# Gate/up pairs 1 to 8 with four seven-product steps, two of their four weight sums on GpSimd, and the last convolution transposes moved inside a step

## The reference

```python
h = rmsnorm(x, norm_mix)
q, k, v, o, i, f, cb, cc, cx, ga, gb = split(h @ w_in)
hm = sigmoid(o) * headnorm(mlstm_chunkwise(q, k, v, i, f)) * mh_norm   # 8 heads, chunks of 128
u = causal_depthwise_conv(cc * cx, conv_w)                             # 3 taps
merged = sigmoid(ga) * (hm @ w_branch_a) + sigmoid(gb) * ((cb * u) @ w_branch_b)
x = x + merged @ w_out
hf = rmsnorm(x, norm_ffn)
x = x + (silu(hf @ w_gate) * (hf @ w_up)) @ w_down                     # w_gate, w_up: 2048 x 5632
out = rmsnorm(x, norm_final)
```

## Time and profile before

| | |
|---|---|
| median of 3 runs | 1713.92 us |
| profiled execution, its own time | 1713.56 us |
| its span, first to last instruction | 1711.7 us |
| TensorE busy | 1698.0 us (99%), 7673 matmuls, granted clock 0.999 |
| VectorE, ScalarE, GpSimd busy | 1281.9, 888.0, 71.3 us |
| gate/up stage | from 1003.6 to about 1470 us of the span |
| DMA | 331.39 MB, mean 194 GB/s |

### The profile page before, as it was taken

The page is one execution under the profiler, slowest core; times in us unless marked ns, Lnnn a source line. Parts: engine busy times, 40 slices in busy tenths (PEclk is TensorE's granted clock), DMA queues, the critical chain, the costliest instruction groups (busy, mean ns, idle before and its releaser), DMA issues.

```text
span 1711.7 us, 20301 instructions
## 1 busy us (share of the span) xinstructions
PE 1698.0 (99%) x7673; PEld 1407.2 (82%) x7673; DVE 1281.9 (75%) x1108; ACT 888.0 (52%) x780; POOL 71.3 (4%) x65
## 2 busy tenths in 40 slices
PE   9999999999999999999999999999999999999998
PEld 7888888888878888888888888888888888888886
DVE  5888555566579998865554589888888888898987
ACT  6555544454455555553333465555555555665564
POOL 1000010101030000000000000000000000230000
PEclk9999999999999999999999999999999999999999
DMA  8555545554546555555556556665556655556653
GB/s 284 187 196 197 195 158 189 172 162 162 181 158 221 197 201 209 206 187 187 189 192 226 197 167 204 199 200 198 201 199 199 199 197 196 187 194 221 221 193 115
DMA packets 139185, 331.39 MB, mean 194 GB/s; under 512 B 8721, under 2 KB 8817, under 8 KB 138737
## 3 DMA queue, kind: packets, MB, share of 16 engines
q1 hardware_dynamic: 138976, 329.98, 57.2%
q10 hardware_dynamic: 144, 0.52, 0.1%
HBM read 328.38 MB, written 2.10 MB: 193 GB/s over the span
## 4 chain that ended last, share of the span: by engine, by line
PE 97%; DVE 1%; issue 1%; ACT 0%; DMA 0%; SPq 0%; POOLq 0%; DVEq 0%; POOL 0%; ACTq 0%
PE ps L1713 11%; PE ps L1714 11%; PE ps L1722 11%; PE ps L2032 9%; PE ps L2034 9%; PE ps L2038 9%; PE ps L1821 7%; PE ps L1814 7%; PE ps L1815 7%; PE ps L2113 4%; PE ps L2114 4%; PE ps L2118 4%; PE ps L1739 1%; PE ps L1988 1%; DVE w_lo L1064 0%
## 5 line engine op out<-in xcount | busy, mean ns | idle before, releaser
L1064 DVE TENSOR_TENSOR w_lo<-w_raw,w_hi 128x2048 fp32r<-128x2048 f32 x308 | 709.2, 2306 | 136.9 <-ACT w_hi L616 134.5
L616 ACT ACTIVATE w_hi<-w_raw 128x2048 fp32r<-128x2048 f32 (+1 forms) x309 | 588.8, 1909 | 291.2 <-PE ps L1714 102.8
L1713 PE MATMUL ps<-w_hi,xT_hi 128*128 128x512 f32 x448 | 179.6, 401 | 1.7 <-ACT w_hi L616 1.7
L1714 PE MATMUL ps<-w_hi,xT_lo 128*128 128x512 f32 x448 | 174.6, 390 | 0.0
L1814 PE MATMUL ps<-w_hi,xT_hi 128*128 128x512 f32 x426 | 165.9, 389 | 0.9 <-ACT w_hi L616 0.9
L1815 PE MATMUL ps<-w_hi,xT_lo 128*128 128x512 f32 x426 | 165.7, 389 | 0.0
L2032 PE MATMUL ps<-w_hi,fT_hi 128*128 128x512 f32 x396 | 156.2, 395 | 0.0
L2034 PE MATMUL ps<-w_hi,fT_lo 128*128 128x512 f32 x396 | 154.3, 390 | 0.0
L616 ACT ACTIVATE t_hi<-t_raw 128x1536 fp32r<-128x1536 f32 x45 | 66.9, 1486 | 110.3 <-PE ps L2038 87.8
L2038 PE MATMUL ps<-w_lo,fT_hi 128*128 128x512 f32 x396 | 120.1, 389 | 0.0
L1821 PE MATMUL ps<-w_lo,xT_hi 128*128 128x512 f32 x426 | 112.5, 390 | 0.4 <-DVE w_lo L1064 0.4
(11 more groups left out here) (344 smaller groups left out, 2801.9 us busy)
## 6 DMA issues: line engine op xcount, KB each, us to landing
w_raw<-in_w_in SPq DMA_DIRECT2D x127, 1024.0 KB, 5.0
w_raw<-in_w_gate SPq DMA_DIRECT2D x88, 512.0 KB, 3.8
w_raw<-in_w_up SPq DMA_DIRECT2D x88, 512.0 KB, 4.6
w_raw<-in_w_down SPq DMA_DIRECT2D x44, 1024.0 KB, 5.1
w_raw<-in_w_branch_b SPq DMA_DIRECT2D x16, 1024.0 KB, 5.2
w_raw<-in_w_branch_a SPq DMA_DIRECT2D x16, 1024.0 KB, 5.1
w_raw<-in_w_out SPq DMA_DIRECT2D x16, 1024.0 KB, 5.3
xn<-in_x SPq DMA_DIRECT2D x4, 512.0 KB, 8.6
```

Of the source, the lines that this page charges most:

```text
L616: copy = lambda o, i, **kw: nc.scalar.activation(o, i, ACT.Copy, **kw)
L1064: V.tensor_tensor(w_lo[:, chunk.split, :], w_raw[:, chunk.raw, :], w_hi[:, chunk.split, :].bitcast(F32), ALU.subtract).then_inc(lo_split, 1)
L1713: T.matmul(ps[:, banks + r, :], rows(hi, k, r), w, start=(q == 0 and k == 0), stop=False)
L1714: last = T.matmul(ps[:, banks + r, :], rows(lo, k, r), w, start=False, stop=False)
```

## The change

- `STEPS` becomes two tables. Pairs 0, 9 and 10 keep the old one (`EDGE`). Pairs 1 to 8 (`INNER`) have "S" at steps 1, 3, 5 and 7, so four steps of seven products where there were three. The activation sums for one more block (`forms6`) are made in pair 0.
- In the inner pairs the weight sums of the first and third "S" step (steps 1 and 5) are made by GpSimd, those of the second and fourth (steps 3 and 7) by VectorE. There are two buffers for the sums, `t_raw` and `t_raw_b`, used in turn.
- The last step of an inner pair is now an "S" step. It runs the three extra products (P1, P6, P7) first, the two VectorE additions of them (`u_sums`) come after the split of the next pair's first chunk, and TensorE starts the next pair with the bank that is free (Q4), waiting for each of the others when it comes to it.
- The last `turn_p` is issued in the middle of the high part of `front_step`, after 4 of its 8 products, and no more after the step.
- SyncE's loop over the pairs and TensorE's last two pairs are written out.

```diff
-STEPS = "ssSsSsSs"
-PAIR_OF = (0, 2, 3, 1, 4, 6, 5, 7)
-LAST_S = 6
+EDGE = ("ssSsSsSs", (0, 2, 3, 1, 4, 6, 5, 7))
+INNER = ("sSsSsSsS", (0, 3, 1, 4, 2, 5, 7, 6))
+INNER_PAIRS = range(1, 9)
+POOL_TURNS = (0, 2)
...
+            def weight_sums(i, n):
+
+                j = S_AT[INNER][n]
...
+                pool.wait_ge(pair_landed[c.raw], 32 * (j // RAW_SLOTS + 1) + i * 64)
+                pool.wait_ge(t_lo_done, sums_free(i, n))
+                nc.gpsimd.tensor_tensor(out=sums[:, 0:2, :], in0=raw[:, 0:1, :].to_broadcast([P, 2, COLS]),
+                                        in1=raw[:, 1:3, :], op=ALU.add).then_inc(pool_t_step, 1)
+                pool.wait_ge(pool_t_step, done + 1)
+                nc.gpsimd.tensor_tensor(out=raw[:, 0, :], in0=sums[:, 0, :], in1=raw[:, 2, :],
+                                        op=ALU.add).then_inc(pool_t_step, 1)
+                pool.wait_ge(pool_t_step, done + 2)
+                nc.gpsimd.tensor_tensor(out=sums[:, 2, :], in0=raw[:, 0, :], in1=raw[:, 3, :],
+                                        op=ALU.add).then_inc(pool_t_step, 1)
+
+            with pool.Fori(INNER_PAIRS[0], INNER_PAIRS[-1] + 1) as i:
+                for n in POOL_TURNS:
+                    weight_sums(i, n)
...
-                    if j in (FIRST_S, FIRST_S + 2):
-                        weight_sums(j + 2, i)
+                    if j in (tab_s[0], tab_s[0] + 2, tab_s[0] + 4) and j + 2 in tab_s:
+                        n = tab_s.index(j + 2)
+                        if tab == EDGE or n not in POOL_TURNS:
+                            weight_sums(i, n)
...
                         pair_split(0, i + 1)
-                        weight_sums(FIRST_S, i + 1)
+                        if tab == INNER:
+                            u_sums(i, banks)
+                        elif table(i + 1) == EDGE or 0 not in POOL_TURNS:
+                            weight_sums(i + 1, 0)
...
-                for name, t, u in parts:
+                for n, (name, t, u) in enumerate(parts):
+                    if n == 4 and midway is not None:
+                        midway()
...
-                    front_step(p, j)
-                    if p == FRONT and j == 0:
-                        turn_p(NB - 1)
+                    front_step(p, j, midway=(lambda: turn_p(NB - 1)) if p == FRONT and j == 0 else None)
```

More of the change, by code:

```diff
@@ L491, in load_down @@
                              w_down_k[:, k:k + 2, col:col + 2 * COLS]).then_inc(raw_landed[chunk.raw], 16)
-            with sp.Fori(0, FB) as i:
+            for i in range(FB):
                 load_pair(i)
@@ L888, in pair_split @@
                 c = Chunk(G_FFN + j, i, 2 * BC)
-                if STEPS[j] == "s":
+                if j not in S_AT[table(i)]:
                     split(c, (pair_landed[c.raw], 32 * (j // RAW_SLOTS + 1) + i * 64))
                     return
[L892 to L898, removed]
+                n = S_AT[table(i)].index(j)
+                summed = sums_landed(i, n)
+                act.wait_ge(*summed)
+                if n > 0:
+                    act.wait_ge(lo_used, Chunk(G_FFN + S_AT[table(i)][n - 1], i, 2 * BC).count(1))
+                elif not starts(i):
+                    act.wait_ge(lo_used, Chunk(G_FFN + S_AT[table(i - 1)][-1] - 2 * BC, i, 2 * BC).count(1))
+                copy(t_hi[:], (t_raw_b if in_b(i, n) else t_raw)[:].rearrange("p u n -> p (u n)")).then_inc(t_hi_done, 1)
+                split(c, summed)
             def f_high(b, turned, halves=1, at_half=0):
@@ L948, in silu, with first_out @@
                                      scale=r_x[:, 1, r:r + 1]).then_inc(silu_done, 1)
+            def first_out(i, banks):
+                if not starts(i):
+                    act.wait_ge(dve_out, V_FFN + i)
+                if starts(i):
+                    act.wait_ge(x1_rstd, 1)
+                copy(c_gate[:, 0, :], ps[:, banks["P1"], :]).then_inc(p1_out, 1)
             def ffn_turn(i, odd, last=False):
@@ L953, in ffn_turn @@
                 for j in range(2 * BC):
[L954 to L960, removed]
+                    if j == 2 * BC - 1 and table(i) == EDGE:
+                        act.wait_ge(lo_used, Chunk(G_FFN + S_AT[EDGE][-1], i, 2 * BC).count(1))
+                        first_out(i, banks)
                     if j < 2 * BC - 1:
@@ L967, in ffn_turn @@
                         pair_split(0, i + 1)
+                    if j == 2 * BC - 1 and table(i) == INNER:
+                        act.wait_ge(extra_done, (i - INNER_PAIRS[0]) * 3 + 1)
+                        first_out(i, banks)
                     if not first and j == 0:
@@ L976, in ffn_turn @@
                         forms_high(1, form_raw1, FORM_AT[1], FORM_AT[2] - FORM_AT[1])
+                    if first and j == 3:
+                        act.wait_ge(form6_step, 3)
+                        copy(form6[0][:], form_raw1[:, 12:15, :]).then_inc(form6_hi_done, 1)
             def stage(c):
@@ L1529, in swiglu, with forms6 @@
                 done.then_inc(dve_out, 1)
+            def forms6():
+                a, b = f_raw[1], f_raw[3]
+                s1, s2, s4 = (form_raw1[:, 12 + k, :] for k in range(3))
+                V.tensor_tensor(s1, a[:, 2, P:2 * P], b[:, 2, P:2 * P], ALU.subtract).then_inc(form6_step, 1)
+                dve.wait_ge(form6_step, 1)
+                V.tensor_tensor(s2, s1, a[:, 2, 0:P], ALU.subtract).then_inc(form6_step, 1)
+                dve.wait_ge(form6_step, 2)
+                V.tensor_tensor(s4, s2, b[:, 2, 0:P], ALU.add).then_inc(form6_step, 1)
@@ new lines, in u_sums @@
+            def u_sums(i, banks):
+                dve.wait_ge(p1_out, i + 1)
+                if starts(i):
+                    dve.wait_ge(x1_rstd, 1)
+                else:
+                    dve.wait_ge(act_turned, i * 2)
+                inner = table(i) == INNER
+                if inner:
+                    dve.wait_ge(extra_done, (i - INNER_PAIRS[0]) * 3 + 2)
+                V.tensor_tensor(c_up[:, 0, :], ps[:, banks["P6"], :], c_gate[:, 0, :],
+                                ALU.add).then_inc(u_step, 1)
+                dve.wait_ge(u_step, i * 2 + 1)
+                if inner:
+                    dve.wait_ge(extra_done, (i - INNER_PAIRS[0]) * 3 + 3)
+                V.tensor_tensor(c_gate[:, 1, :], ps[:, banks["P7"], :], c_up[:, 0, :],
+                                ALU.add).then_inc(u_step, 1)
@@ L1531, in ffn_turn @@
             def ffn_turn(i, odd, last=False):
                 first = starts(i)
+                tab, tab_s = table(i), S_AT[table(i)]
                 banks = pair_banks(odd)
                 for j in range(2 * BC):
[L1535 to L1545, removed]
@@ L1582, in ffn_turn @@
                 add(4, c_gate[:, 1, :], "Q4", c_gate[:, 1, :], ALU.add)
+                if tab == INNER and not last and (table(i + 1) == EDGE or 0 not in POOL_TURNS):
+                    weight_sums(i + 1, 0)
             def stage(c):
@@ L2003, in tile_of @@
                     return f[:, c + KC // 2 * (int(name[2]) - 1), r * P:(r + 1) * P]
+                if c == 6 and name[0] == "S":
+                    return form6[part][:, ("S1", "S2", "S4").index(name), :]
                 g, k = c // KB, c % KB
@@ L2041, in pair_step @@
                 pe.wait_ge(hi_split, c.count(1))
-                if STEPS[j] == "S":
-                    pe.wait_ge(t_hi_done, T_FRONT + S_BEFORE[j] + i * S_TURNS + 1)
+                if j in tab_s:
+                    pe.wait_ge(t_hi_done, t_turn(i, tab_s.index(j)) + 1)
                 if j == 2 * BC - 1:
+                    if j in tab_s:
+                        for part in parts[0:3]:
+                            high(part)
+                        pe.wait_ge(lo_split, c.count(1))
+                        for part in parts[0:3]:
+                            low(part).then_inc(extra_done, 1)
                     pe.wait_ge(lo_split, c.count(1))
-                    for name in dict.fromkeys(p[0] for p in parts):
+                    for name in ("P2", "Q5", "Q3", "Q4"):
                         for part in own(name):
@@ L2055, in pair_step @@
                 for part in parts:
+                    if j == 0 and not starts(i) and part is own(part[0])[0]:
+                        if part[0] == "P2":
+                            pe.wait_ge(p1_out, i)
+                        if part[0] == "Q5":
+                            pe.wait_ge(u_step, i * 2 - 1)
+                        if part[0] == "Q3":
+                            pe.wait_ge(u_step, i * 2)
                     last = high(part)
@@ L2070, in ffn_turn @@
                         pe.wait_ge(form_lo_done, 1)
-                    if first and j == FIRST_S:
+                    if first and j == 2:
                         pe.wait_ge(dve_out, V_FFN)
@@ L2075, in ffn_turn @@
                         pe.wait_ge(form_lo_done, 2)
-                    if not first and j == 0:
-                        pe.wait_ge(u_step, i * 2)
```

(4 more changed lines are left out.)

113 lines of the change are left out of this document (81 added, 32 removed).

## The result

The changed kernel takes 1732.4 us (median of 4 runs, 1731.8 to 1733.6), the kernel before in the same session 1714.18 us: a ratio of 1.0108, 95% interval 1.0094 to 1.0122. It is 18.2 us slower. 1727.0 us was predicted, with 1711 to 1738 as the range, so the forecast was 5.4 us too low.

What follows compares the result with a forecast made beforehand. The prediction took TensorE, 97% of the chain that ended last, as the bound. Matmuls removed (-5.4), transposes (-1.6) and GpSimd-caused waits (+20.5) gave +13.5 on 1713.56: 1727.0 us, range 1711 to 1738.

Steps and rivals of the forecast that it cites:

- Matmuls removed: Inner pairs: three matmuls fewer in each of 8, 5.44 us; a pair without waits takes 41.76 us.
- Last transposes: End of the convolution: transposes start 3.6 us earlier, recovering 1.6 us of TensorE's 1.67 us standing near 503 and 507.
- GpSimd's own length, and the holding: Inner-pair sums: GpSimd takes 2.36 us for 1024 elements, 1.28 for 512, holding VectorE's two-SBUF-operand work 2.2 and 1.1.
- One sign: Expected in the new trace: GpSimd's 1024 elements take 2.4 us where VectorE idles, up to 4.6 elsewhere.
- A steady inner pair: Gate/up stage: 44.5 us a pair on VectorE, from work 35.2, held 7.5, idle 1.8; TensorE waits 2.7.
- the wait in step 7: Inner pairs: TensorE waits 0.5 us for `w_lo` of step 7.
- The sum, +13.5: Whole kernel: -5.4 - 1.6 + 20.5 on the profiled execution's 1713.56, giving 1727.0 us.
- the likeliest case: Whole kernel: 2.0 to 3.5 us of waits per pair, 1721 to 1733 us; chance 0.65.
- the spare time would first be used up in pair 1: Pair 1: spare time delays the waits there; with no GpSimd set behind pair 8, 7.5 pairs were counted.
- the worse rival: Slot 1 lands over 1.35 us later, step 7's `t_lo` goes first: pairs 45.8 us, time 1737; chance 0.11.
- Edits at nothing: `forms6`, the added `t_hi`, SyncE's loads and step 7's new order cost nothing; `forms6` would cost 1.2 us without cover.
- The faster one: GpSimd's additions fall into VectorE's idle time and PSUM additions, up to 4.8 us held per pair: 1706.6 us; chance 0.15.

Runs made afterwards that it cites:

- the additions: Kernel with the early sums plus unread GpSimd additions of SBUF constants, four of 512 elements at each of the change's two times: 1772.36 us, ratio 1.0341.
- the memsets: Kernel with the early sums plus eight unread GpSimd memsets of 512 elements per set in place of the four additions: 1710.89 us, ratio 0.9981.
- the kernel with the early sums: The change with all sums on VectorE, the next pair's first set made before the `t_lo` of step 7: 1710.79 us, ratio 0.9983.
- the run with all sums on VectorE: The change with GpSimd's sums moved to VectorE, first set behind the main additions, VectorE's pair loop written out: 1740.62 us, ratio 1.0155.

## Why the prediction was right

**Matmuls removed, 5.4 us.** Right in size: 7673 became 7649. With VectorE free of GpSimd, inner pairs are 41.76 to 42.1 us apart, against 41.76 worked out.

**Last transposes, 1.6 us.** Right: in the kernel with this edit alone ScalarE's copy starts at 483.29 (483.0 worked out). From the low part at 501.27 to the next step's low part at 506.25 are 4.98 us, where they were 507.75 - 500.99 = 6.76: 1.78 less. The 2.1 us between medians agree with 1.67 within the interval.

**GpSimd's own length, and the holding.** Right: 2.36 us for 1024 elements, 2.40 measured, and 1.28 for 512, 1.29 measured; a hold of 2.2 and 1.1 us, where `t_lo` grew by 3.96 - 1.75 = 2.21 and by 2.79 - 1.75 = 1.04. Two `w_lo` grew by 6.69 - 4.55 = 2.1. The shared port pair of the Trainium skill (SBUF — State Buffer, section "SBUF: two separate sides") stands behind this, and so does its clause that VectorE operations with two SBUF inputs are held only against a GpSimd operation that reads SBUF: the additions cost 61.6 us, the memsets none. One sign was read too high: beside a busy VectorE, GpSimd's 1024 elements take 2.6 to 3.3 us in step 3, not 4.6, because they meet the end of a `w_lo` and not its start.

**A steady inner pair, 44.5 us.** The places were right to half a microsecond or a little more; the sum was 0.5 short. From X = 1203.15, the end of `w_lo` of step 3 (TensorE goes on at 1203.18): GpSimd starts at X+12.9 (12.4 predicted), `t_lo` of step 7 at X+14.15 (13.75), the main additions end at X+27.9 (27.3), `w_lo` of step 2 at X+37.8 (37.3), the next X comes at X+45.05. The first 0.4 us has arisen by that `t_lo`: TensorE's own time from X to the end of step 5 was taken at 0.2267 us a matmul, 12.3 us. It took 12.6, because the last matmul (1215.35) is 0.39 us long and ScalarE waits for its end (0.16), and because the first matmul after the transposes is followed only 0.32 us later (1205.26 to 1205.58). ScalarE's copy was 0.04 us longer than taken.

The term that was sized too small is the wait in step 7. Counted by matmul starts against the 0.2267 us pace, TensorE loses 1.7 us in step 3 (1.7 predicted), 1.2 in step 7 (0.5) and 0.4 in step 2 (0.5). The waits view shows less, 1.4, 0.75 to 0.91 and at most 0.16 in most pairs, since it counts from the modelled end of the last matmul and leaves out that after a wait the second start comes 0.34 us behind the first (1203.18 to 1203.52). That is also why its 18.3 us are less than the loss below.

**The sum, +13.5.** The direction and the mechanism held; the term of waits was too small, 20.5 us for 25.2. From the transposes of pair 1 to those of pair 10 the changed kernel needs 1463.89 - 1062.13 = 401.76 us, the kernel before 382.02: 19.7 more, to which the 5.4 us of removed matmuls come. Pairs 1 to 7 lose 3.2 to 3.3 us each against 41.76, but for the second, which loses 4.0 (its raw slot landed later and step 7 waited 1.64 us), and pair 8 loses 1.7. I had 2.7 in 7.5 pairs. That the spare time would first be used up in pair 1 was wrong: it waits 1.41 us in step 3 at once (at 1067.36). The remaining 0.4 us of the profiled execution's 20.1 lies outside: the 1.8 us won at the transposes were lost again elsewhere. 1.1 us of that had been lost ahead of any edited instruction (the low part at 502.13, in the kernel before at 500.99); this execution waited 1.0 us for `w_hi` at 17.30. Of two executions of the kernel with the early sums one has such a wait and one has not, so it does not belong to the change. The other 0.9 us was lost between there and pair 1, some 0.3 of it at the wait in pair 0 named below; the rest stays open.

The measured 1732.4 is at the upper edge of the likeliest case's 1721 to 1733 and as near to the worse rival's 1737. The time alone would not have told these two apart; the trace does.

**Edits at nothing.** Right for the new order of step 7 and of the banks: no wait for `t_hi` or a bank shows in any run. Nearly right for `forms6`: pair 0 has one new wait for `w_lo`, 0.23 us at 1028.67, and the kernels without GpSimd have it too; no run has `forms6` alone. My remark that the sums taken off VectorE would give 0.9 us a pair was about its work only. Where those sums stand decides more: behind the main additions they cost waits of 2.7 to 4.0 us a pair by way of ScalarE's `w_hi`, which I did not see before the run with all sums on VectorE.

**The rivals.** The faster one asked for under 4.8 us held per pair; it was 7.5 (1.04 + 2.14 and 2.21 + 2.14). The worse one did not come about: the raw slot landed at X+12.9 and ahead of the `t_lo`. Pair 2 went part of that way: GpSimd started 0.5 us before `t_lo`, which took 3.52 us.

## What to carry to other kernels

In this kernel GpSimd was no free hand beside a VectorE that is nearly full of operations with two SBUF operands: charge each of its SBUF-reading operations to VectorE in full, less what falls into VectorE's idle time or its PSUM additions, before comparing with the work taken off. Then lay the remaining work in the order in which the engine behind needs it: here VectorE had idle time all along, 1.8 us ahead of one split, and moving the sums into it gave what moving them to another engine did not. When a helper's result is needed by a third engine, follow that engine's queue too.

## What the runs showed of the hardware

After the longest waits TensorE ran slower for a while. In the run with all sums on VectorE, the granted clock is the third number from the end of each row (columns as in the earlier trace rows); the stretches are before the wait, the wait, and two after it:

```profile
1230.00:1234.80 4.80, 4.80 (x23) 3.94 (x21) 4.28 (x6) 0.36 (x1) 0.00 (x0) 1.00 0.49 180
1234.80:1239.15 4.35, 0.37 (x3) 0.01 (x1) 1.86 (x2) 4.32 (x4) 0.00 (x0) 0.79 0.00 0
1239.15:1244.30 5.15, 5.15 (x12) 4.07 (x13) 5.12 (x5) 4.31 (x4) 0.00 (x0) 0.51 0.34 91
1244.30:1250.00 5.70, 5.70 (x26) 4.70 (x25) 4.97 (x5) 3.30 (x2) 0.00 (x0) 1.00 0.50 158
```

The engine had stood 3.98 us; then 12 matmuls start 0.43 us apart, which is the lower level (1.2 GHz), until 1244, at an extra cost of about 2.4 us on top of the wait. That is the longest such stretch of this run. After its other two waits of 4.0 us 7 or 8 matmuls are slow (1.5 us), and the same after two of its four waits of 2.7 us; twice the slow stretch begins only some matmuls after the wait, as at 1193.0 behind the wait that ended at 1191.51. After the other two waits of 2.7 us, and after every wait of the changed kernel (at most 1.6 us), matmuls start at full speed. So the price of one and the same wait differs from pair to pair, and these runs do not show what decides it.

The 24.0 us of waits and about 8.6 us for the 43 slow matmuls make 32.6 us, near what the spans show: the profiled executions of this kernel and of the one with the early sums are 1741.2 - 1709.2 = 32.0 us apart. The medians are 29.8 apart; the profiled execution was the slowest of this kernel's four.
